# Two of eight routed experts run in a packed form with two matrix products a group, and GpSimd makes some of their weights' low parts

## The chip, the cores and the metric

One core of one Trainium2 chip runs the kernel. The metric is the device time in microseconds (us) of the slowest core, here the only one. The kernel before took 1445.33 us (median of 3 runs, 1445.06 to 1445.63). Engines are named as in the profile: PE multiplies matrices (PEld loads its stationary operand), DVE is VectorE, ACT is ScalarE, POOL is GpSimd, and SP issues most transfers.

## The reference

The reference is a two-layer decoder trunk: 256 tokens, model width 1024, all in float32. The change touches its last block, a feed-forward layer with eight experts of which each token takes two:

```python
logits = (x @ w_router).astype(jnp.float32)
top_logit, top_idx = lax.top_k(logits, 2)
gates = jax.nn.softmax(top_logit, axis=-1)
# for each expert e, over the tokens routed to it:
y = (jax.nn.silu(h @ w_gate[e]) * (h @ w_up[e])) @ w_down[e]
# w_gate, w_up: 1024 x 3584, w_down: 3584 x 1024, for each expert
out = zeros.at[rows_token].add(y * gate)      # then residual and a final rmsnorm
```

512 assignments fall on eight experts, 64 each on average. With the reference's own inputs (seed 0) the counts are 67, 51, 56, 55, 77, 75, 59 and 72. The order in which experts are worked on does not change the result, except for rounding.

## The kernel before

Every float32 weight is used as two parts that PE reads in a faster float32 form: `e_whi`, the rounded value, and `e_wlo`, the remainder. Activations are split in the same way. A product is then three matmuls, high x high, low x high and high x low (`three`, L1688 to L1690).

The weights of an expert come in 42 slots of 1 MB. Seven steps j handle 512 hidden columns each: two slots for the gate projection, two for the up projection and two for the down projection of the step before. A slot goes through a line of four:

- SP issues the load into one of 7 buffers `raw` (L440, L455); it waits until the low part of the slot 7 places earlier is done (`lo_ready`).
- ACT copies the slot into one of 6 buffers `e_whi` (L979), once PE has used the slot 6 places earlier.
- DVE subtracts and writes `e_wlo` (L1569).
- PE does 12 matmuls of 512 columns with it.

The order on each engine is written out by hand in its own block of code; semaphores tie the engines together. In a step PE does the gate product of step j, turns the hidden rows of step j-1 (`turn_hidden`, L2310), does the up product of step j and then the down product of j-1. ACT does the silu (L1002) and the high part of the turned hidden rows (L984), DVE the product gate x up (L1619) and their low part (L1582).

Up to 128 tokens of an expert sit in the 128 columns of the stationary operand. SP fetches an expert's tokens from `routed_rows` in DRAM during step 5 of the expert before (L449), PE turns them (L2304). POOL computes where each token's row goes, scatters the rows by indirect transfers (L551), stores each expert's result in `y_rows` (L559), and near the end gathers the rows of each token back (L568); DVE adds those, weighted, to the residual `xres` (`add_rows`, L1538). The last expert's result goes from PE's accumulator through a one-hot product (L2388) straight into `xres` (L1673), and the final norm follows. Where an expert has over 128 tokens a second pass over all experts runs; with these inputs it does not.

Of the kernel before, what the change touches and what calls it, by code (L numbers as in the profile page):

```python
# [24 lines left out]
P = 128  # L25
# [18 lines left out]
E_SPLIT = 6  # L44

# [53 lines left out]
def trunk(nc, x, mem, g_mix, g_ffn, w_mem_kv, w_out, w_in_a, w_gk_up, b_gk, g_gla, g_kv, w_kv, w_in_b,  # L99
# [10 lines left out]
    with ExitStack() as ctx:  # L110
# [15 lines left out]
        sb("act_pad", [P, 24])  # L126
# [12 lines left out]
        w_all = sb("w_r", [P, 184])[:, 0:KT * NE]  # L139
        w_r = w_all.rearrange("p (k e) -> p k e", k=KT)  # L140
        LOGITS = slice(NE * (KT - 1), NE * KT)

# [32 lines left out]
        h_hi, h_lo = ([buf[:, 4 * i:4 * i + 4, P:S] for i in range(2)] for buf in (act_hi, act_lo))  # L175

# [10 lines left out]
        y_mark = small[0:1, 28:29]  # L187
        cur_rank, cur_gate = small[:, 76:78], small[:, 78:80]
# [101 lines left out]
        ranked = sem("ranked")  # L290
# [23 lines left out]
        e_silu = sem("e_silu")  # L314
        e_hr = sem("e_hr")
        e_tr = sem("e_tr")
# [96 lines left out]
        def _(sp):  # L413
# [17 lines left out]
            def expert_loads(sweep):  # L431
                base = NPRE + sweep * NE * PER_EXPERT
                with sp.Fori(0, NE) as e:
                    u = 0
                    for j in range(STEPS + 1):
                        for wgt in ((w_exp_gate, w_exp_up) if j < STEPS else ()):
                            for half in range(2):
                                s = base + u
                                sp.wait_ge(lo_ready, e * PER_EXPERT + s - RAW + 1)
                                sp.dma_start(shaped(raw, s % RAW, 4, 512),  # L440
                                             wgt[0, e].rearrange("(k p) n -> p k n", p=P)
                                             [:, 4 * half:4 * half + 4, 512 * j:512 * j + 512])\
                                  .then_inc(raw_in[s % RAW], 16)
                                u += 1
                        if sweep == 0 and j == 5:
                            sp.wait_ge(rows_sent, 16 * 2 * TT)
                            sp.wait_ge(copy_sent, 16 * TT)
                            sp.wait_ge(disp, 2 * e + 2)
                            sp.dma_start(x_rows, routed_rows[P:].rearrange("(e p) d -> e p d", p=P)[e])\  # L449
                              .then_inc(x_rows_in, 16)  # L450
                        for half in (range(2) if j > 0 else ()):
                            s = base + u
                            sp.wait_ge(lo_ready, e * PER_EXPERT + s - RAW + 1)
                            k0 = 4 * (j - 1) + 2 * half
                            sp.dma_start(shaped(raw, s % RAW, 2, D),  # L455
                                         w_exp_down[0, e].rearrange("(k p) n -> p k n", p=P)[:, k0:k0 + 2, :])\
                              .then_inc(raw_in[s % RAW], 16)
                            u += 1

            expert_loads(0)  # L460
            sp.wait_ge(routed, 1)
            over = sp.value_load(flag[0:1, 0:1], min_val=0, max_val=S)
# [16 lines left out]
        def _(pool):  # L479
# [45 lines left out]
            pool.wait_ge(ranked, 1)  # L525
            iota8 = cst[:, C_IOTA:C_IOTA + NE].rearrange("p (o e) -> p o e", o=1).to_broadcast([P, TT, NE])
            nc.gpsimd.tensor_scalar(row1, route_rank[:, :, :], P - 0.5, 1.0e6, ALU.is_gt, ALU.mult)
            link(nc.gpsimd.tensor_scalar(row_of, iota8, float(P), None, ALU.mult))
# [27 lines left out]
            nc.gpsimd.tensor_copy(y_idx, rsc[:, 6:8, :, 0].rearrange("p c t -> p t c")).then_inc(y_idx_ready, 1)  # L556
            for i in range(NE - 1):
                pool.wait_ge(e_yo, 2 * (i + 2))
# [4 lines left out]
            pool.dma_start(gain[:, :], gains[-1].to_broadcast([P, D])).then_inc(gain_in, 16)  # L563
            pool.wait_ge(y_idx_ready, 1)
            for t in range(TT):
                pool.wait_ge(lo_ready, NPRE + NE * PER_EXPERT - RAW + t + 1)
                for c in range(2):
                    pool.indirect_dma_start(y_back[t][:, c, :], None, y_rows[:, :],  # L568
                                            bass.IndirectOffsetOnAxis(ap=y_idx[:, t, c:c + 1], axis=0),
                                            bounds_check=NE * P - 1, oob_is_err=True).then_inc(y_in[t], 16)  # L570

# [5 lines left out]
        def _(act):  # L577
# [384 lines left out]
            def evacuate_rows(i):  # L962

                act.wait_ge(slot_used, i * PER_EXPERT + NPRE)
                act.wait_ge(y_free, i + 1)
                for n in range(2):
                    ns = slice(512 * n, 512 * n + 512)
                    nc.scalar.activation(y_tok[:, ns], ps[:, 5 + n, :], ACT.Copy).then_inc(e_yo, 1)

            def experts(sweep):  # L970
# [16 lines left out]
                def expert(e, last):  # L987

                    for j in range(STEPS):
# [8 lines left out]
                        if j == 2 and (sweep or last):  # L998
                            act.wait_ge(oh_turned, e + 2 if sweep else 1)
                            nc.scalar.activation(ohT[:, :], ps[:, 7, 0:256], ACT.Copy).then_inc(ohT_ready, 1)  # L1000
# [10 lines left out]

                split_slots(0, 0, 1)
# [31 lines left out]
        def _(dve):  # L1044
# [434 lines left out]
            link(nc.vector.memset(flag[:, :], 0))  # L1479
            out_b_sums(0)  # L1480
# [26 lines left out]
            nc.vector.memset(rt[:, 30:31], 0.0).then_inc(ranked, 1)  # L1507

            def choice_inverse():
# [5 lines left out]
                link(nc.vector.tensor_reduce(rt[:, 24:25], ps[:, 4, 0:NE], AX.X, ALU.max))  # L1515
                nc.vector.tensor_copy(flag[0:1, 0:1], rt[0:1, 24:25]).then_inc(routed, 1)
# [14 lines left out]

            def add_rows(t, c):

                dve.wait_ge(gated, 1)
                dve.wait_ge(y_in[t], 32)
                if c:
                    dve.wait_ge(y_added, 2 * t + 1)
                nc.vector.scalar_tensor_tensor(out=xres[:, t, :], in0=y_back[t][:, c, :],  # L1538
                                               scalar=rt[:, 4 + 2 * c + t:5 + 2 * c + t], in1=xres[:, t, :],
                                               op0=ALU.mult, op1=ALU.add).then_inc(y_added, 1)  # L1540

            def experts(sweep):
# [45 lines left out]
                def expert(e, last):  # L1588

                    for j in range(STEPS):  # L1590
# [29 lines left out]
                        if j == STEPS - 1 and sweep == 0 and last:  # L1620
                            add_rows(0, 0)
# [5 lines left out]
                    hidden(e, STEPS - 1)  # L1627
                    if not last:
                        split_slots(e, PER_EXPERT + 1, 1)
                        gathered(sweep, e + 1)  # L1630
# [11 lines left out]
                with dve.Fori(0, NE - 1) as e:  # L1642
                    expert(e, False)
                expert(NE - 1, True)
                return remainder_y, add_tile

            remainder_y, add_tile = experts(0)
            add_rows(0, 1)
            add_rows(1, 0)
            add_rows(1, 1)  # L1650
            dve.wait_ge(routed, 1)
            over = dve.value_load(flag[0:1, 0:1], min_val=0, max_val=S)
            last_gates = cur_gate.rearrange("p (t o) -> p t o", o=1)
            with dve.If(over > P):
                remainder_y(NE)
                nc.vector.tensor_copy(last_gates, route_gate[:, :, NE:NE + 1]).then_inc(cur_done, 1)
# [5 lines left out]
            nc.vector.tensor_copy(last_gates, route_gate[:, :, NE:NE + 1]).then_inc(last_gate, 1)  # L1662
# [5 lines left out]
            dve.wait_ge(last_gate, 1)  # L1668
            for n in range(2):
# [15 lines left out]
        def _(pe):  # L1685
# [570 lines left out]
            def experts(sweep):  # L2256
# [49 lines left out]

                def turn_hidden(e, j):
# [30 lines left out]
                def expert(e, last):  # L2338
                    for j in range(STEPS):
# [8 lines left out]
                        if j == 2 and (sweep or last):  # L2348
                            pe.wait_ge(oh_ready, 2 * e + n_oh + 2 if sweep else 4)
# [6 lines left out]
                        elif j == 0:  # L2356
                            pe.wait_ge(routed, 1)
# [14 lines left out]
                with pe.Fori(0, NE - 1) as e:  # L2372
                    expert(e, False)
                expert(NE - 1, True)
# [3 lines left out]
            over = pe.value_load(flag[0:1, 0:1], min_val=0, max_val=S)  # L2378
# [58 lines left out]
```

## Time and profile before

| | us |
|---|---|
| median of 3 runs | 1445.33 |
| the profiled execution | 1445.62 |
| its span | 1443.8 |
| PE busy | 1416.1 (98%) |
| DVE busy | 1116.0 (77%) |
| ACT busy | 944.2 (65%) |
| POOL busy | 52.9 (4%) |
| DMA, mean | 309 GB/s |

The span is the stretch that the profile shows, 1.8 us less than the execution's own time. The expert stage runs from about 486 us to 1434 us. "Busy" of matmuls is modelled and overlaps, so the distance between the same place in two experts or steps says more than the busy sum.

### The profile page before, as it was taken

How to read it: one execution, taken by the hardware profiler on the slowest of the kernel's cores; microseconds unless marked ns; L12 is line 12 of the kernel's file. 1: busy time of each engine (PE TensorE's matmuls, PEld its weight loads, DVE VectorE, ACT ScalarE, POOL GpSimd, SP SyncE). 2: the span in 40 equal slices, each digit the busy share in tenths (PEclk: the TensorE clock that was granted, in tenths of full speed). 3: DMA queues.
4: the chain of work that ended last, by engine and by line, in shares of the span. 5: the costliest groups of instructions: out<-in, count | busy, mean ns of one | idle time of the engine just before them, and what ended most of it. 6: DMA issues, size and time to landing. Idle time of an engine off the chain costs nothing.

```text
span 1443.8 us, 19619 instructions
## 1 busy us (share of the span) xinstructions
PE 1416.1 (98%) x7392; PEld 1201.2 (83%) x7392; DVE 1116.0 (77%) x865; ACT 944.2 (65%) x866; POOL 52.9 (4%) x78
## 2 busy tenths in 40 slices
PE   9999999999999999999999999999999999999997
PEld 8887899998888888888888888888888888888886
DVE  4565544556776899798888889879889888988987
ACT  5654543434664877786777777767768767677773
POOL 1000100000000500000000000000000000000002
PEclk9999999999999999999999999999999999999999
DMA  9843675555531699999999999999999999999993
GB/s 278 270 146 118 238 243 177 194 185 189 190 117 59 236 396 396 397 393 395 394 361 397 394 346 392 398 345 388 397 392 351 395 393 345 393 398 363 392 397 128
DMA packets 205254, 446.72 MB, mean 309 GB/s; under 512 B 8449, under 2 KB 42401, under 8 KB 205201
## 3 DMA queue, kind: packets, MB, share of 16 engines
q1 hardware_dynamic: 200144, 428.34, 80.6%
q0 software_dynamic: 5056, 17.66, 3.6%
q8 instruction: 35, 0.57, 0.2%
q14 instruction: 19, 0.15, 0.0%
HBM read 432.86 MB, written 13.11 MB: 309 GB/s over the span
## 4 chain that ended last, share of the span: by engine, by line
PE 91%; ACT 3%; DVE 3%; DMA 1%; issue 0%; DVEq 0%; SPq 0%; ACTq 0%
PE ps L1688 29%; PE ps L1690 29%; PE ps L1689 29%; PE ps L2310 2%; DMA raw<-in_w_in_a_dram 1%; ACT w_hi L595 1%; DVE w_lo L1060 1%; PE ps L1839 0%; PE ps L1714 0%; PE ps L2304 0%; DVE small L1107 0%; ACT sc L639 0%; DVE act_lo L1073 0%; DMA H<-in_mem_dram 0%; PE ps L1823 0%
## 5 line engine op out<-in xcount | busy, mean ns | idle before, releaser
L1569 DVE TENSOR_TENSOR e_wlo<-raw,e_whi 128x2048 fp32r<-128x2048 f32 x336 | 752.0, 2284 | 102.2 <-ACT e_whi L979 102.1
L979 ACT ACTIVATE e_whi<-raw 128x2048 fp32r<-128x2048 f32 x336 | 622.5, 1915 | 48.7 <-PE ps L1690 27.6
L1688 PE MATMUL ps<-e_whi,act_hi 128*128 128x512 f32 x1344 | 529.4, 394 | 1.3 <-DVE act_lo L1527 1.3
L1690 PE MATMUL ps<-e_wlo,act_hi 128*128 128x512 f32 x1344 | 523.9, 390 | 0.0
L1689 PE MATMUL ps<-e_whi,act_lo 128*128 128x512 f32 x1344 | 523.2, 389 | 0.0
L1690 PEld LDWEIGHTS ps<-e_wlo,act_hi 128*128 128x128 f32 x1344 | 252.3, 188 | 53.4
L1688 PEld LDWEIGHTS ps<-e_whi,act_hi 128*128 128x128 f32 x1344 | 252.4, 188 | 52.5 <-DVE act_lo L1527 1.9
L1689 PEld LDWEIGHTS ps<-e_whi,act_lo 128*128 128x128 f32 x1344 | 252.6, 188 | 50.7
L1060 DVE TENSOR_TENSOR w_lo<-raw,w_hi 128x2048 fp32r<-128x2048 f32 (+3 forms) x69 | 148.7, 2167 | 119.8 <-ACT w_hi L595 119.5
L595 ACT ACTIVATE w_hi<-raw 128x2048 fp32r<-128x2048 f32 (+3 forms) x69 | 124.3, 1816 | 49.6 <-PE ps L1690 43.8
L984 ACT ACTIVATE act_hi<-ps 128x512 fp32r<-128x512 f32 x56 | 33.5, 599 | 158.7 <-PE ps L2310 158.7
L1688 PE MATMUL ps<-act_hi,w_hi 128*128 128x256 f32 (+2 forms) x440 | 124.8, 284 | 2.5 <-DVE act_lo L1073 2.5
L1689 PE MATMUL ps<-act_hi,w_lo 128*128 128x256 f32 (+2 forms) x440 | 124.3, 282 | 0.0
L1690 PE MATMUL ps<-act_lo,w_hi 128*128 128x256 f32 (+2 forms) x440 | 124.3, 282 | 0.0
L1688 PE MATMUL ps<-w_hi,act_hi 128*128 128x512 f32 (+1 forms) x272 | 98.9, 364 | 6.1 <-DVE act_lo L1073 4.2
L1690 PE MATMUL ps<-w_lo,act_hi 128*128 128x512 f32 (+1 forms) x272 | 96.0, 353 | 0.0
L1689 PE MATMUL ps<-w_hi,act_lo 128*128 128x512 f32 (+1 forms) x272 | 95.7, 352 | 0.0
L1688 PEld LDWEIGHTS ps<-act_hi,w_hi 128*128 128x128 f32 (+2 forms) x440 | 81.8, 186 | 3.9 <-issue 3.4
L1689 PEld LDWEIGHTS ps<-act_hi,w_lo 128*128 128x128 f32 (+2 forms) x440 | 81.8, 186 | 0.5
L1690 PEld LDWEIGHTS ps<-act_lo,w_hi 128*128 128x128 f32 (+2 forms) x440 | 81.8, 186 | 0.2
L1688 PEld LDWEIGHTS ps<-w_hi,act_hi 128*128 128x128 f32 x272 | 51.4, 189 | 14.7 <-DVE act_lo L1073 2.4
L1690 PEld LDWEIGHTS ps<-w_lo,act_hi 128*128 128x128 f32 x272 | 51.4, 189 | 7.3
(270 smaller groups left out, 967.3 us busy)
## 6 DMA issues: line engine op xcount, KB each, us to landing
raw<-in_w_exp_gate_dram SPq DMA_DIRECT2D x112, 1024.0 KB, 8.7
raw<-in_w_exp_up_dram SPq DMA_DIRECT2D x112, 1024.0 KB, 9.1
raw<-in_w_exp_down_dram SPq DMA_DIRECT2D x112, 1024.0 KB, 9.8
raw<-in_w_dense_gate_dram SPq DMA_DIRECT2D x11, 1024.0 KB, 5.4
raw<-in_w_dense_up_dram SPq DMA_DIRECT2D x11, 1024.0 KB, 5.8
raw<-in_w_dense_down_dram SPq DMA_DIRECT2D x11, 1024.0 KB, 6.3
raw<-in_w_out_dram SPq DMA_DIRECT2D x8, 1024.0 KB, 5.1
raw<-in_w_in_a_dram SPq DMA_DIRECT2D x7, 1024.0 KB, 12.2
```

What stands on the lines that cost most here:

```text
L595: nc.scalar.activation(w_hi[:, s % SPLIT, 0:kt * n], raw[:, s % RAW, 0:kt * n], ACT.Copy)\
L979: nc.scalar.activation(e_whi[:, (s - NPRE) % E_SPLIT, :], raw[:, s % RAW, :], ACT.Copy)\
L984: nc.scalar.activation(h_hi[j % 2], ps[:, 4, :].rearrange("p (m n) -> p m n", m=4), ACT.Copy)\
L1060: nc.vector.tensor_tensor(w_lo[:, s % SPLIT, 0:kt * n], raw[:, s % RAW, 0:kt * n], w_hi[:, s % SPLIT, 0:kt * n].bitcast(F32), ALU.subtract)\
L1569: nc.vector.tensor_tensor(e_wlo[:, r, :], raw[:, s % RAW, :], e_whi[:, r, :].bitcast(F32), ALU.subtract).then_inc(lo_ready, 1)
L1688: nc.tensor.matmul(dst, l_hi, r_hi, start=start, stop=False)
L1689: nc.tensor.matmul(dst, l_lo, r_hi, start=False, stop=False)
L1690: return nc.tensor.matmul(dst, l_hi, r_lo, start=False, stop=stop)
L2310: ins = nc.tensor.transpose(ps[:, 4, P * m:P * m + P], e_h[:, P * m:P * m + P], ident)
```

## The change

- Experts are put in order of their token count: expert 0 first, then by falling count, so that the two with the fewest tokens come last (indices 6 and 7 in this order, `FIRST_LIGHT = 6`). POOL computes the order from the counts; SP reads an expert's number from it before it loads that expert.
- These two "light" experts have room for 64 tokens (`LIGHT = 64`). The stationary operand holds the high parts of 64 tokens and beside them their low parts. One matmul with the weights' high part and one with their low part then give all four partial products; a group has 2 matmuls where it had 3. The two halves of the result lie in different rows and are added by a product with `fold`, two identity blocks on top of each other.
- Since silu needs the sum, ACT and DVE first copy gate and up unchanged (`light_gate`, `light_up`), PE folds and turns both in 8 small matmuls (`light_turn`), and silu, product and split come behind it on 256 columns.
- In steps 1 to 5 of a light expert POOL makes the low part of the step's fourth slot (the second of the down projection, slot `gate_end(j) + 3`). DVE waits for it and passes `lo_ready` on, to keep the order.
- The weighted adds of the gathered rows move from DVE to POOL, as a scaling and an add each, 8 instructions behind the last gather.
- Each engine has its own code for the light experts instead of the loop's.
- A count above 64 in a light expert, or above 128 elsewhere, starts the second pass.

The core of the diff:

```diff
+ # SP, sweep 0
+ loads(0, 0)
+ sp.wait_ge(routed, 1)
+ with sp.Fori(1, NE) as e:
+     loads(e, sp.value_load(order_of[0:1, bass.ds(e, 1)], min_val=0, max_val=NE - 1))
+ # POOL: before the row numbers; ranked was signalled by DVE ahead of its first weight slot
- pool.wait_ge(ranked, 1)
+ pool.wait_ge(counted, 1)
+ link(nc.gpsimd.tensor_scalar(key[:, :], count[:, :], float(NE), None, ALU.mult))
...
+ nc.gpsimd.tensor_copy(flag[0:1, 0:1], past[0:1, 0:1]).then_inc(routed, 1)
...
+ def low_parts(e):
+     for j in range(1, STEPS - 1):
+         s = NPRE + e * PER_EXPERT + gate_end(j) + 3
+         r = (s - NPRE) % E_SPLIT
+         pool.wait_ge(hi_ready, s + 1)
+         nc.gpsimd.tensor_tensor(e_wlo[:, r, :], raw[:, s % RAW, :], e_whi[:, r, :].bitcast(F32), ALU.subtract)\
+           .then_inc(pool_lo, 1)
...
+ # POOL, at the very end
+ for t in range(TT):
+     pool.wait_ge(y_in[t], 32)
+     for c in range(2):
+         nc.gpsimd.tensor_scalar(y_back[t][:, c, :], ..., ALU.mult).then_inc(y_scaled, 1)
+         nc.gpsimd.tensor_tensor(xres[:, t, :], xres[:, t, :], y_back[t][:, c, :], ALU.add).then_inc(y_added, 1)
+ # ACT, a step of a light expert
+ split_slots(e, up, 2)
+ split_slots(e, up + 2, 1)
+ light_silu(e, j - 1)
+ light_gate(e, j)
+ light_high(e, j - 1)
+ split_slots(e, up + 3, 2)
+ split_slots(e, up + 5, 1)
+ # DVE, a step of a light expert (passed_on waits for POOL's slot)
+ split_slots(e, up, 2)
+ light_product(e, j - 1)
+ split_slots(e, up + 2, 1)
+ light_low(e, j - 1)
+ passed_on(e, j)
+ light_up(e, j)
+ split_slots(e, up + 4, 2)
+ # DVE, before the last additions to xres
+ dve.wait_ge(y_added, 2 * TT)
+ # PE, a slot of a light expert
+ for kk in range(4):
+     k = 4 * half + kk
+     nc.tensor.matmul(bank, xg_hi[:, k, :], hi[:, kk, :], start=k == 0, stop=False)
+     ins = nc.tensor.matmul(bank, xg_hi[:, k, :], lo[:, kk, :], start=False, stop=k == KT - 1)
+ # PE, between the last two experts: the result of the light expert before is folded
+ def fold_rows():
+     pe.wait_ge(y_raw, 2)
+     for n in range(2):
+         ins = nc.tensor.matmul(ps[0:LIGHT, 5 + n, :], fold, y_tok[:, 512 * n:512 * n + 512], start=True, stop=True)
```

DVE in the last expert, before: a step is six `e_wlo`, one `act_lo` and one `e_h`, and the adds to `xres` come behind the last step.

```order
L1569 TENSOR_TENSOR e_wlo<-raw,e_whi 128x2048 [waits hi_ready] x2
L1619 TENSOR_TENSOR e_h<-e_h,ps 128x512 [waits slot_used,e_silu]
L1569 TENSOR_TENSOR e_wlo<-raw,e_whi 128x2048 [waits hi_ready] x4
L1582 TENSOR_TENSOR act_lo<-ps,act_hi 128x4x128 [waits e_hi]
L1569 TENSOR_TENSOR e_wlo<-raw,e_whi 128x2048 [waits hi_ready] x2
L1619 TENSOR_TENSOR e_h<-e_h,ps 128x512 [waits slot_used,e_silu]
L1538 SCALAR_TENSOR_TENSOR xres<-raw,small,xres 128x1024 [waits y_in0,gated]
```

DVE in a light expert, after (`H` holds the up product and the folded rows; the MEMSET is `passed_on`):

```order
L1713 TENSOR_TENSOR e_wlo<-raw,e_whi 128x2048 [waits hi_ready]
L1775 TENSOR_TENSOR act_hi<-H,act_hi 128x4x64 [waits e_hi]
L1799 MEMSET small 1x1 [waits pool_lo]
L1795 COPY H<-ps 128x512 [waits slot_used]
L1713 TENSOR_TENSOR e_wlo<-raw,e_whi 128x2048 [waits hi_ready] x4
L1771 TENSOR_TENSOR H<-H,ps 128x256 [waits l_silu]
L1713 TENSOR_TENSOR e_wlo<-raw,e_whi 128x2048 [waits hi_ready]
L1775 TENSOR_TENSOR act_hi<-H,act_hi 128x4x64 [waits e_hi]
L1799 MEMSET small 1x1 [waits pool_lo]
```

One of six `e_wlo` has left DVE, and in its place stands a wait for POOL, with the copy of the up product and all later slots behind it. POOL from the gather to its end, after (before, the four gathers were the last; `raw` and `xres` are what they fill and what is added to):

```order
L639 TENSOR_TENSOR e_wlo<-raw,e_whi 128x2048 [waits hi_ready] x5
L656 DMA raw<-y_rows,idx 128x1024 [waits lo_ready,y_idx_ready]
L656 DMA raw<-y_rows,idx 128x1024
L656 DMA raw<-y_rows,idx 128x1024 [waits lo_ready]
L656 DMA raw<-y_rows,idx 128x1024
L662 TENSOR_SCALAR raw<-raw,small 128x1024 [waits y_in0]
L665 TENSOR_TENSOR xres<-xres,raw 128x1024 [waits y_scaled]
L662 TENSOR_SCALAR raw<-raw,small 128x1024 [waits y_added]
L665 TENSOR_TENSOR xres<-xres,raw 128x1024 [waits y_scaled]
L662 TENSOR_SCALAR raw<-raw,small 128x1024 [waits y_in1,y_added]
```

The additions now stand in one line on POOL, each behind the one before. POOL's routing before its scatter of the rows, which had 13 instructions from `ranked` on, has 43 from `counted` on; nearly all wait for the one ahead of them.

## Rows read from the trace of the kernel before

**Rows 1.** The page, parts 2 and 4: GB/s in 40 slices; shares of the chain.

```profile
GB/s 278 270 146 118 238 243 177 194 185 189 190 117 59 236 396 396 397 393 395 394 361 397 394 346 392 398 345 388 397 392 351 395 393 345 393 398 363 392 397 128
...
PE 91%; ACT 3%; DVE 3%; DMA 1%; issue 0%; DVEq 0%; SPq 0%; ACTq 0%
```

**Rows 2.** Busy time by stretch: one expert; DVE's `e_wlo` line alone.

```profile
700.00:818.60 118.60, 118.60 (x542) 98.09 (x541) 103.03 (x59) 86.24 (x60) 0.67 (x2) 1.00 1.02 385
...
487.20:546.00 58.80, 51.95 (x24) 1.00 1.02 384
```

**Rows 3.** The page, part 5: count, busy us, mean ns of one, idle before and its releaser.

```profile
L1569 DVE TENSOR_TENSOR e_wlo<-raw,e_whi 128x2048 fp32r<-128x2048 f32 x336 | 752.0, 2284 | 102.2 <-ACT e_whi L979 102.1
L979 ACT ACTIVATE e_whi<-raw 128x2048 fp32r<-128x2048 f32 x336 | 622.5, 1915 | 48.7 <-PE ps L1690 27.6
```

**Rows 4.** The chain that ended last: start us, us, what.

```profile
568.00 0.44 PE ps L2310 x4
...
1189.92 0.87 PE ps L2304 x8
...
1308.56 0.87 PE ps L2304 x8
1331.21 0.44 PE ps L2310 x4
1348.01 0.44 PE ps L2310 x4
```

**Rows 5.** Timeline of DVE: start us, us, line, operation, count, idle before and its releaser.

```profile
487.28 4.51 DVE L1569 TENSOR_TENSOR e_wlo<-raw,e_whi 128x2048 fp32r<-128x2048 f32 x2
...
1204.16 4.49 DVE L1569 TENSOR_TENSOR e_wlo<-raw,e_whi 128x2048 fp32r<-128x2048 f32 x2 [6.34 <-ACT e_whi L979]
...
1390.23 8.89 DVE L1569 TENSOR_TENSOR e_wlo<-raw,e_whi 128x2048 fp32r<-128x2048 f32 x4
...
1418.83 4.49 DVE L1569 TENSOR_TENSOR e_wlo<-raw,e_whi 128x2048 fp32r<-128x2048 f32 x2 [1.60 <-ACT e_whi L979]
...
1434.23 2.73 DVE L1673 SCALAR_TENSOR_TENSOR xres<-ps,small,xres 128x512 f32<-128x512 f32 x4
```

**Rows 6.** Timeline of ACT: the wait at the start of the seventh expert, the last copies.

```profile
1201.73 0.60 ACT L1002 ACTIVATE e_h<-ps 128x512 f32<-128x512 f32 x1 [4.27 <-PE ps L1690]
...
1432.86 0.60 ACT L1038 ACTIVATE y_hi<-ps 128x512 fp32r<-128x512 f32 x1 [0.70 <-PE ps L1690]
```

**Rows 7.** Timeline of POOL.

```profile
482.57 0.79 POOL L535 TENSOR_TENSOR rsc<-rsc 128x16 f32<-128x16 f32 x3
...
489.73 2.15 POOL L546 TENSOR_TENSOR route_gate<-rsc 128x16 f32<-128x16 f32 x1
...
497.91 2.50 POOL L551 DMA_INDIRECT routed_rows<-H,idx  x1 [0.30 <-issue]
...
1407.41 2.88 POOL L568 DMA_INDIRECT raw<-y_rows,idx  x1 [83.67 <-DVE e_wlo L1569]
...
1414.91 1.90 POOL L568 DMA_INDIRECT raw<-y_rows,idx  x1 [0.30 <-issue]
```

**Rows 8.** Groups of POOL by line and shape: count, busy us, mean ns of one.

```profile
L503 POOL MEMSET T<- 128x1024 f32 x1 | 1.0, 974 | 0.0
...
L532 POOL TENSOR_TENSOR rsc<-rsc 128x16 f32<-128x16 f32 x1 | 0.2, 227 | 0.0
...
L544 POOL TENSOR_TENSOR small<-small 128x2 f32<-128x2 f32 x1 | 0.2, 197 | 0.0
```

**Rows 9.** Timeline of SP's queue: the row fetch in the first expert.

```profile
548.72 2.31 SPq L449 DMA_DIRECT2D H<-routed_rows  x1
```

**Rows 10.** Lines L551, L568 and L455 by themselves: time from issue to landing.

```profile
DMA to landing us min/median/max: 7.5/9.0/9.4
...
DMA to landing us min/median/max: 5.5/5.8/6.8
...
DMA to landing us min/median/max: 4.9/9.8/15.4
```

More of the change, by code:

```diff
@@ L432, in expert_loads, with loads @@
                 base = NPRE + sweep * NE * PER_EXPERT
-                with sp.Fori(0, NE) as e:
+                def loads(e, x):
                     u = 0
@@ L1627, in expert, with light_product, light_low @@
                     hidden(e, STEPS - 1)
+                    if not last:
+                        split_slots(e, PER_EXPERT + 1, 1)
+                        gathered(sweep, e + 1)
+                def light_product(e, j):
+                    dve.wait_ge(l_silu, (e - FIRST_LIGHT) * STEPS + j + 1)
+                    nc.vector.tensor_tensor(h_T, s_T, ps[:, 4, 256:512], ALU.mult).then_inc(l_prod, 1)
+                def light_low(e, j):
+                    dve.wait_ge(e_hi, e * STEPS + j + 1)
+                    nc.vector.tensor_tensor(h_hi[j % 2][:, :, LIGHT:P], h_T.rearrange("p (m n) -> p m n", m=4),
+                                            h_hi[j % 2][:, :, 0:LIGHT].bitcast(F32), ALU.subtract).then_inc(e_lo, 1)
@@ new lines, in light_up, with passed_on, light_expert @@
+                def light_up(e, j):
+                    dve.wait_ge(slot_used, e * PER_EXPERT + base + gate_end(j) + 2)
+                    nc.vector.tensor_copy(e_u, ps[:, 2 + j % 2, :]).then_inc(e_hr, 1)
+                def passed_on(e, j):
+                    dve.wait_ge(pool_lo, (e - FIRST_LIGHT) * (STEPS - 2) + j)
+                    nc.vector.memset(y_mark2, 0.0).then_inc(lo_ready, 1)
+                def light_expert(e, last):
+                    for half in range(2):
+                        pack(e, half)
+                    split_slots(e, 2, 2)
+                    if last:
+                        light_one_hot()
+                    split_slots(e, 4, 2)
+                    light_up(e, 0)
+                    for j in range(1, STEPS):
+                        up = gate_end(j)
+                        split_slots(e, up, 2)
+                        light_product(e, j - 1)
+                        split_slots(e, up + 2, 1)
+                        light_low(e, j - 1)
+                        if j < STEPS - 1:
+                            passed_on(e, j)
+                        else:
+                            split_slots(e, up + 3, 1)
+                        light_up(e, j)
+                        split_slots(e, up + 4, 2)
+                    if not last:
+                        split_slots(e, PER_EXPERT, 1)
+                    light_product(e, STEPS - 1)
+                    light_low(e, STEPS - 1)
@@ L2347, in expert @@
                             scatter(e + 1, 1)
[L2348 to L2349 removed]
+                        if j == 2 and sweep:
+                            pe.wait_ge(oh_ready, 2 * e + n_oh + 2)
                             for t in range(TT):
```

270 lines of the change are left out of this document (219 added, 51 removed).

## The prediction

> **What bounds the kernel now.** I read the chain of waits first: PE holds 91% of it, and within the experts it is only matmuls [rows 1, 4]. The same turn of token rows stands at 1189.92 and 1308.56, so an expert takes 118.64 us; two hidden turns are 16.80 us apart, which is a step of six slots [rows 4]. The turn is 0.44 us of it, so a matmul comes every (16.80 - 0.44) / 72 = 0.227 us and a slot costs PE 12 x 0.227 = 2.73 us. The busy time by stretch comes next, to see who is second: in one expert of 118.6 us DVE is busy 103.0 and ACT 86.2, POOL 0.7, and 385 GB/s are moved [rows 2]. The slices of the page stand at about 396 GB/s wherever no expert begins [rows 1]; at that pace a 1 MB slot takes 2.65 us. So four engines work at nearly one pace: PE 2.73 us a slot, DMA 2.65, DVE 2.28, ACT 1.92 [rows 3]. Taking a third of PE's work away can win little before another takes over; the question is which, and what it does.
>
> **PE's part.** A light slot has 8 matmuls, 1.81 us, 0.92 less. Over 84 slots that is 77 us, but it does not reach the end: a step would be 10.9 us on PE plus a fold, and neither DMA (15.9 us) nor DVE allows it. DVE alone with six slots would need 6 x 2.2 (back to back four take 8.89 [rows 5]) plus the copy of up (0.6, a little under 2.73 / 4 as in the last additions [rows 5]), product and low part on 256 columns (0.4 each, estimated from 0.6 on 512), together 14.6. DMA would then set the pace, under the present 16.8.
>
> **The slot that POOL takes.** Here the order on the engines decides. DVE can't run ahead of its wait in `passed_on`. I follow one cycle from the end of `light_product`: ACT may now do `light_high` (0.4) and only then the copy of the slot that POOL is to work on (1.9); with a handoff 2.4 us. POOL's subtraction takes P, and 0.2 goes for its two handoffs. Then DVE copies up (0.6), makes four `e_wlo` (8.85) and the next product (0.4). DVE's one slot and `light_low` in between (2.6) fit beside ACT's 2.4, so POOL's P stands open on DVE. The cycle is 2.4 + 0.2 + P + 0.6 + 8.85 + 0.4 = 12.45 + P. PE and SP wait behind DVE.
>
> P is not in the trace: no two-input operation of 2048 elements ran on POOL. From below: a memset of 1024 took 0.974 us, one stream [rows 8], so 1.95 us for 2048. From above: two streams in and one out at that pace, 5.8 us. Between them, two tensor-tensor operations on 16 and on 2 elements took 227 and 197 ns, a slope of 2.1 ns an element, and 4.6 us at 2048. That is the nearest row in kind, though the lever is short; I take 4.4. A cycle is then 16.85 us, where the step of before was 16.80.
>
> The Trainium skill (GPSIMD Engine Reference, "Performance versus the Vector engine") gives 4497 ns for such an addition of 2048 elements on GpSimd against 2293 ns on VectorE. The trace bears out the second with 2284 ns [rows 3] and shows nothing of the first; with it the sum below would be 1 us more.
>
> **Do POOL and DVE wait for each other?** POOL's L546 is a 16-element operation that takes 2.15 us and ends at 491.88, just behind the pair of `e_wlo` that ends at 491.79, while three such operations in a gap of DVE took 0.79 together [rows 5, 7]. So a POOL operation is held for as long as DVE's two-input one. Whether a long one on POOL holds DVE equally no row shows. In the cycle it matters little, as DVE is waiting anyway; at the end it does.
> The Trainium skill (SBUF — State Buffer, "The single rule") says it goes both ways, whichever starts first: by that rule the slot given away costs DVE more than it saves, in any order of the instructions.
>
> **The sum**, along DVE. Seventh expert: slots 4 and 5 began at 1204.16, behind ACT's wait for PE's first two slots [rows 5, 6]; PE is 2 x 0.92 faster, so 1202.35. Two `e_wlo` 4.45, up 0.6, two more 4.4, product 0.4: 1212.2. Five cycles of 16.85: 1296.45. To slot 41: 2.2 + 0.4 + 2.2 + 0.6 + 4.45 = 9.85, so 1306.3. The same place before is 1423.32 - 118.64 = 1304.7 (end of the last pair [rows 5]). Eighth: slot 0 2.2, product 0.4, ACT's high part and copy 2.4, slot 1 2.2, gathered rows 1.2, pack 0.25 make 8.65. Then the fold stands in the way: PE's four slots 7.25 and the two folding matmuls (in plain float32; between 0.45 as fast ones and four times that; I take 1.8), ACT's evacuation 1.1, its next copy 1.9, handoffs 0.3, then two `e_wlo` 4.45, up 0.6, two 4.4 and product 0.4: 30.85 in all, where before the same stretch takes 27.6 (1204.16 + 4.45 + 0.6 + 4.45 + 118.64 - 1304.7). That is 1337.15; five cycles, 1421.4; 9.85, 1431.25. POOL's first tail operations hold the last two slots for 1.4: 1432.65, against 1423.32 before.
>
> **The end.** PE is close behind now: product, high, low and handoffs 1.5, two slots 3.6, one hold by POOL 1.2, so 6.3 us after that slot, and the last additions could start 1.7 later (1434.23 against 1432.55 before [rows 5, 6]), 8.0 in all. But they now wait for POOL's additions. The gathers start 15 us before the last slot is done (six slots and the small ones), take 9.4 to issue as 1407.41 to 1416.81, and the first pair lands 5.8 after its second issue [rows 7, 10], some 5.5 us before the last slot. Then four scalings (1.0 from the memset) and four additions (P/2 = 2.2), handoffs 0.8 and two `e_wlo` ahead of them (4.4) make 18.0: 12.5 us behind the last slot, 4.5 later than PE's side. Before, DVE did them under PE's matmuls. Additions start at 1432.65 + 12.5 = 1445.15, before at 1434.23: 10.9 later. The rest stays as it is.
>
> **The routing on POOL.** 43 chained operations begin only at 487.2, with DVE on `e_wlo` in 51.95 of the next 58.8 us [rows 2]. One gets through with each of the 23 or so slots; a gap of DVE takes one to three, at 0.26 to 0.3 each [rows 7]. That ends near 546. The scatter's last issue comes 6.0 behind them (497.91 - 491.88) and lands 9.4 later [rows 7, 10]: 561, where SP asked for the rows at 548.72 [rows 9]. The weight load behind it lands at 562.8 + 4.9 [rows 10], its low part is done at 572.3, and PE wants it after the turn at 568.00 and two more slots [rows 4], at 573.9. So 12 us of wait are covered with 1.6 us left. I put 1 us down, bounds 0 and 10. The expert number that SP reads costs no more than a few of its idle microseconds once an expert.
>
> Together 10.9 + 1.0 = 11.9 on the profiled execution's 1445.62, which is 0.3 above the median: 1457.5 us.
>
> **The rivals.**
> - POOL's part is cheap. With P = 2.3, as on DVE, ten cycles lose 2.1 each and the four additions 1.05: 1457.5 - 21 - 4.2 = 1432. DMA about permits it: 84 loads and 1.5 more for rows take 226.6 us at 2.65, and DVE's way would be 237.3 + 9.3 - 21 = 225.6. For it: the memset's pace. Against: two inputs, and the slope of the small operations. The sign turns at P = 4.4 - 11.9 / 12 = 3.4.
> - POOL is slower than I take it, or DVE and POOL hold each other in every cycle: 5.8 us gives 1457.5 + 14.0 + 2.8 = 1474. For it: three streams; against: the slope.
> - The routing comes too late. Were each of the 43 operations to wait for a whole DVE slot (2.55 us apart), it would end at 597, the rows land at 612, and PE would stand for 48 us: 1505. It decides from 563 us on (561 + 1.6). For it: only 1.6 us of cover. Against: small operations pass in DVE's gaps, and DVE stops when loads stop.
> - The change doesn't do what it says, because a light expert has over 64 tokens and all eight run twice. The counts of 51 and 55 speak against it; it would be over 2300 us.
>
> **How the numbers follow.** The forecast with its near range (1450 to 1466) has 0.6, the cheap POOL 0.2 (times 1431 to 1442), the slower POOL 0.1, late routing 0.09, the second pass 0.01. The range of 8 in 10 goes from 1438 to 1470. 0.2%, 2.9 us, is about what a measurement of this kernel can tell: faster 0.19, same 0.05, slower 0.76.
>
> **What would show it.** POOL's 2048-element row near 4.4 us, ten of them, each with DVE idle and the wait before the MEMSET put down to POOL; hidden turns of the last two experts about 16.9 us apart; PE idle in them; the last `xres` additions waiting for POOL; SP's row fetch near 561. It is wrong if P is under 3.4 us, if POOL starts while DVE still has slots to do, or if PE stands in the first expert.

## The result and the profile after

The changed kernel takes 1467.47 us (median of 4 runs, 1467.0 to 1468.95), the kernel before 1445.19 in the same comparison (4 runs, 1444.14 to 1445.63). The ratio is 1.0158, with an interval of 1.0142 to 1.0174: 22.3 us slower. The forecast was 1457.5 with a range of 1438 to 1470, so the time lies inside the range, and 1.5 us above the near range of 1450 to 1466 that had a chance of 0.6.

| | before | after |
|---|---|---|
| the profiled execution | 1445.62 | 1467.45 |
| its span | 1443.8 | 1465.6 |
| PE busy | 1416.1 (98%) | 1389.5 (95%) |
| DVE busy | 1116.0 (77%) | 1096.4 (75%) |
| POOL busy | 52.9 (4%) | 165.4 (11%) |

PE has less work and the kernel takes longer, so the time must be in waits. Parts 2 and 4 of the page after the change, beside [rows 1]:

```profile
POOL 1000100000000790000000000000000002211247
...
GB/s 281 260 144 115 277 218 188 202 194 176 170 115 30 328 393 368 393 394 397 391 363 395 395 347 397 393 350 393 398 350 390 397 363 369 374 380 310 364 366 68
...
PE 77%; POOL 6%; DVE 6%; ACT 4%; issue 3%; DMA 3%; SPq 1%; DVEq 0%; ACTq 0%; POOLq 0%
```

PE's share of the chain is 77% where it was 91%. In the slices of the last two experts (363, 369, 374, 380 and on) the transfers no longer reach 396 GB/s.

POOL's groups of the changed kernel (count, busy us, mean ns of one, idle before and its releaser). L639 is the low part, L662 and L665 are the scaling and the addition near the end:

```profile
L639 POOL TENSOR_TENSOR e_wlo<-raw,e_whi 128x2048 fp32r<-128x2048 f32 x10 | 46.3, 4626 | 121.8 <-ACT e_whi L1075 121.8
L662 POOL TENSOR_SCALAR raw<-raw,small 128x1024 f32<-128x1024 f32 x4 | 13.3, 3330 | 0.3
L665 POOL TENSOR_TENSOR xres<-xres,raw 128x1024 f32<-128x1024 f32 x4 | 9.6, 2407 | 0.3
```

P is 4.63 us where [rows 3] have 2.284 for the same work on DVE. The Trainium skill (GPSIMD Engine Reference, "Performance versus the Vector engine") gives 4497 ns for an addition of this size; the subtraction in the trace is 0.13 us above it.

One cycle on DVE in the seventh expert after the change (start us, us, what, idle before), to be held against the steady six `e_wlo` of before:

```profile
1213.14 0.41 DVE L1771 TENSOR_TENSOR H<-H,ps 128x256 f32<-128x256 f32 x1
1213.47 2.29 DVE L1713 TENSOR_TENSOR e_wlo<-raw,e_whi 128x2048 fp32r<-128x2048 f32 x1
1215.67 0.42 DVE L1775 TENSOR_TENSOR act_hi<-H,act_hi 128x256 fp32r<-128x256 f32 x1
1220.56 0.69 DVE L1795 COPY H<-ps 128x512 f32<-128x512 f32 x1 [4.47 <-issue]
1220.58 0.06 DVE L1799 MEMSET small<- 1x1 f32 x1
1221.17 8.89 DVE L1713 TENSOR_TENSOR e_wlo<-raw,e_whi 128x2048 fp32r<-128x2048 f32 x4
1230.61 0.42 DVE L1771 TENSOR_TENSOR H<-H,ps 128x256 f32<-128x256 f32 x1 [0.55 <-ACT H L1110]
```

And what POOL does in the same stretch:

```profile
1215.90 4.63 POOL L639 TENSOR_TENSOR e_wlo<-raw,e_whi 128x2048 fp32r<-128x2048 f32 x1 [10.17 <-ACT e_whi L1075]
1233.37 4.63 POOL L639 TENSOR_TENSOR e_wlo<-raw,e_whi 128x2048 fp32r<-128x2048 f32 x1 [12.85 <-ACT e_whi L1075]
```

POOL begins at 1215.90, just behind DVE's slot (done at 1215.76), and ends at 1220.53; DVE goes on at 1220.56. The profile books these 4.47 us to "issue". That POOL ends 0.03 us before DVE goes on, and 0.04 us before it in the next cycle (1238.00 and 1238.04), shows whose wait it is. POOL itself waits 10 to 13 us in each cycle. So the two engines take turns.

### The profile page after: what moved, and what is told of

Read it like the earlier page. It is cut to its first block, busy times and chain, and to the rows that moved or that the text cites. A ratio compares the mean times of both kernels' runs of the same rounds, so it can differ in the third digit from the quotient of the medians.

```text
span 1465.6 us, 19160 instructions
## 1 busy us (share of the span) xinstructions
PE 1389.5 (95%) x7228; PEld 1170.5 (80%) x7228; DVE 1096.4 (75%) x881; ACT 945.3 (65%) x882; POOL 165.4 (11%) x125
## 4 chain that ended last, share of the span: by engine, by line
PE 77%; POOL 6%; DVE 6%; ACT 4%; issue 3%; DMA 3%; SPq 1%; DVEq 0%; ACTq 0%; POOLq 0%
PE ps L1896 21%; PE ps L1898 21%; PE ps L1897 21%; PE ps L2523 3%; PE ps L2524 3%; DVE e_wlo L1713 3%; PE ps L2545 2%; DMA raw<-in_w_exp_down_dram 2%; PE ps L2547 2%; PE ps L2534 1%; PE ps L2589 1%; DMA raw<-in_w_mem_kv_dram 1%; POOL raw L662 1%; ACT w_hi L691 1%; ACT e_whi L1075 1%
## 5 line engine op out<-in xcount | busy, mean ns | idle before, releaser
L1713 DVE TENSOR_TENSOR e_wlo<-raw,e_whi 128x2048 fp32r<-128x2048 f32 x326 | 733.3, 2297 | 90.4 <-ACT e_whi L1075 90.4
L1896 PE MATMUL ps<-e_whi,act_hi 128*128 128x512 f32 x1008 | 397.2, 394 | 1.6 <-DVE act_lo L1681 1.3
L1898 PE MATMUL ps<-e_wlo,act_hi 128*128 128x512 f32 x1008 | 393.0, 390 | 0.0
L1897 PE MATMUL ps<-e_whi,act_lo 128*128 128x512 f32 x1008 | 392.4, 389 | 0.0
L1896 PEld LDWEIGHTS ps<-e_whi,act_hi 128*128 128x128 f32 x1008 | 189.3, 188 | 40.4 <-DVE act_lo L1681 1.9
L1898 PEld LDWEIGHTS ps<-e_wlo,act_hi 128*128 128x128 f32 x1008 | 189.2, 188 | 40.0
L1897 PEld LDWEIGHTS ps<-e_whi,act_lo 128*128 128x128 f32 x1008 | 189.4, 188 | 38.0
L1080 ACT ACTIVATE act_hi<-ps 128x512 fp32r<-128x512 f32 x42 | 25.1, 598 | 120.4 <-PE ps L2589 120.4
L2523 PE MATMUL ps<-e_whi,act_hi 128*128 128x512 f32 x224 | 93.5, 417 | 7.6 <-DVE e_wlo L1713 7.5
L2524 PE MATMUL ps<-e_wlo,act_hi 128*128 128x512 f32 x224 | 90.5, 404 | 0.0
L2545 PE MATMUL ps<-e_whi,act_hi 128*128 128x512 f32 x112 | 54.3, 485 | 33.0 <-DVE small L1799 24.4
```

The costliest lines, as they stand in the source:

```text
L1080: nc.scalar.activation(h_hi[j % 2], ps[:, 4, :].rearrange("p (m n) -> p m n", m=4), ACT.Copy)\
L1713: nc.vector.tensor_tensor(e_wlo[:, r, :], raw[:, s % RAW, :], e_whi[:, r, :].bitcast(F32), ALU.subtract).then_inc(lo_ready, 1)
L1896: nc.tensor.matmul(dst, l_hi, r_hi, start=start, stop=False)
L1897: nc.tensor.matmul(dst, l_lo, r_hi, start=False, stop=False)
L1898: return nc.tensor.matmul(dst, l_hi, r_lo, start=False, stop=stop)
L2523: nc.tensor.matmul(bank, xg_hi[:, k, :], hi[:, kk, :], start=k == 0, stop=False)
```

## The experiments

### The two parts of POOL's work, each by itself

Three kernels put POOL's parts back on DVE: the low parts, the additions, and both. They and the fourth below ran on one chip beside 13 runs of the kernel before (1444.36 us).

```diff
  # e1_dve_low, and in e3_dve_both: POOL makes no low parts, DVE makes all six
-     if i >= FIRST_LIGHT:
-         low_parts(i)
...
-     if j < STEPS - 1:
-         passed_on(e, j)
-     else:
-         split_slots(e, up + 3, 1)
+     split_slots(e, up + 3, 1)
```
```diff
  # e2_dve_adds, and in e3_dve_both: DVE adds behind its last light_low, POOL's 8 instructions go
-         nc.gpsimd.tensor_scalar(y_back[t][:, c, :], ..., ALU.mult).then_inc(y_scaled, 1)
-         nc.gpsimd.tensor_tensor(xres[:, t, :], xres[:, t, :], y_back[t][:, c, :], ALU.add).then_inc(y_added, 1)
...
+     nc.vector.scalar_tensor_tensor(out=xres[:, t, :], in0=y_back[t][:, c, :], scalar=..., in1=xres[:, t, :],
+                                    op0=ALU.mult, op1=ALU.add).then_inc(y_added, 1)
```

> DVE makes all low parts of the light experts again, one edit; POOL keeps the additions at the end. The order theory (DVE stands for all of POOL's 4.6 us in each of ten cycles of 17.1 us): a cycle falls to what DVE needs by itself, 14.6 to 14.9 us, so DVE's last slot comes 22 to 24 us earlier, POOL's additions then end some 18 us behind it, and the time is 1445 to 1449 us. The rival, that transfers set the pace once POOL is out (six slots of 2.65 us, 15.9 a cycle): some 12 us are won, 1453 to 1457 us. If the fallen matmul clock set the cycle: no change of the hidden turns' distance from 17.1 us, 1465 us or more.

> DVE makes the four weighted additions behind its last low part, as before the change; POOL keeps its ten low parts. The theory that POOL's chain at the end costs 6.3 us behind PE (its additions end at 1456.0, PE's side could start them at 1449.7) and 2.1 us more by holding DVE's last two low parts (8.03 us for both instead of 4.49): 8 us less, 1458 to 1461 us. The rival, that the gathers are late anyway because POOL comes to them late: the additions wait for the second pair of rows, and only 2 to 4 us are won, 1463 to 1466 us.

> Both edits: POOL has neither low parts nor additions, the two-product form of the light experts stays. If the two costs stand one behind the other and DVE's own order sets the cycle (14.6 to 14.9 us): 22 to 24 and 8 us less than the changed kernel, 1431 to 1438 us, faster than the kernel before. If transfers set the pace (15.9 us a cycle): 1445 to 1449 us. If the two-product form itself were what is slow (fold, clock, waits at the experts' start), it would stay above 1450 us.

| kernel | low parts | additions | us, median | ratio, interval |
|---|---|---|---|---|
| changed | POOL | POOL | 1467.47 | 1.0158, 1.0142 to 1.0174 |
| e2_dve_adds | POOL | DVE | 1457.48 | 1.0080, 1.0063 to 1.0097 |
| e1_dve_low | DVE | POOL | 1450.91 | 1.0044, 1.0027 to 1.0061 |
| e3_dve_both | DVE | DVE | 1442.90 | 0.9987, 0.9977 to 0.9996 |

Taken away from the changed kernel, the low parts on POOL are worth 1.14% (16.5 us) and the additions 0.78% (11 us); both together 1.71% (25 us), which is less than the sum of the two, so they overlap by some 3 us. With neither the change is 1.9 us faster than before by the ratio, with an interval of 0.6 to 3.3 us. So the two things given to POOL carry the whole loss, and the low parts the larger half. e1_dve_low came out between the two expectations, e2_dve_adds a little below its own, e3_dve_both at neither: 5 us above the one by DVE's order, 2 us below the one by transfers.

DVE in e3_dve_both, cycles without POOL:

```profile
1228.37 0.42 DVE L1768 TENSOR_TENSOR H<-H,ps 128x256 f32<-128x256 f32 x1
...
1242.88 0.42 DVE L1768 TENSOR_TENSOR H<-H,ps 128x256 f32<-128x256 f32 x1
...
1257.42 0.42 DVE L1768 TENSOR_TENSOR H<-H,ps 128x256 f32<-128x256 f32 x1
...
1273.67 0.42 DVE L1768 TENSOR_TENSOR H<-H,ps 128x256 f32<-128x256 f32 x1 [1.68 <-ACT H L1099]
```

A cycle between two products takes 14.51 us here, as the 14.6 of the prediction; POOL's slot made it 17.47 in the rows above. Ten cycles at this pace would save some 26 us. But only the first three cycles of an expert run at it; in the seventh expert the fourth takes 16.25 and the fifth 15.87, in the eighth 15.63 and 16.07. All ten take 151.1 us where those of the changed kernel take 171.0, those of e1_dve_low 152.8, and of the 18.2 us won there 16.5 reach its end. The waits of ACT between 1220 and 1420 us in e3_dve_both (us in total, times, longest) say where the rest is:

```profile
ACT H L1099 <- PE ps L2532: 15.2, 7, 3.6
ACT e_whi L1064 <- DMA raw<-in_w_exp_down_dram: 11.7, 10, 2.3
ACT e_whi L1064 <- DMA raw<-in_w_exp_up_dram: 6.4, 10, 0.8
ACT gain L1053 <- PE ps L2555: 4.9, 1, 4.9
ACT e_whi L1064 <- DMA raw<-in_w_exp_gate_dram: 3.5, 6, 0.8
```

Three of the lines are loads that arrive too late, 21.6 us in all. The chain of waits says the same: from 1332 to 1420 us a third of it (33.0%) is transfers of `raw`, such as

```profile
1376.34 12.68 DMA raw<-in_w_exp_down_dram
```

and the changed kernel's chain has no transfer in that stretch. From 1220 to 1300 us 395 GB/s are moved, before's pace. So, by the trace, transfers set the pace once DVE doesn't. The first line is ACT's wait for the fold and turn of each step, and no run tells how much of it hangs on the loads. The line on `gain` is the fold between the experts, taken up below.

### Do DVE and POOL run at the same time?

In the changed kernel DVE stands while POOL works. Here DVE copies up and makes the next slot's low part first, and waits for POOL after that.

```diff
  # e4_one_ahead: DVE, steps 1 to 5 of a light expert
-     passed_on(e, j)
-     light_up(e, j)
-     split_slots(e, up + 4, 2)
+     light_up(e, j)
+     one_ahead(e, j)          # the low part of slot gate_end(j) + 4, then the wait for POOL
+     split_slots(e, up + 5, 1)
```

> POOL keeps its low parts, but DVE copies up and makes the next slot's low part before it waits for POOL, so that this work could run beside POOL's. If a two-input operation of DVE is held for as long as POOL's runs: only the copy of up (0.6 us, from PSUM) is won in each of ten cycles, 1460 to 1463 us, and the low part that stands ahead starts only when POOL's ends. If DVE and POOL can run together: 2.8 us a cycle, down to the transfers' 15.9 us a cycle or below, 1440 to 1456 us.

It took 1499.49 us, ratio 1.0375 (1.0357 to 1.0392). DVE and POOL in one cycle (L1808 is the subtraction that was moved ahead):

```profile
1235.20 0.42 DVE L1773 TENSOR_TENSOR H<-H,ps 128x256 f32<-128x256 f32 x1 [3.88 <-ACT H L1112]
...
1239.72 5.03 DVE L1808 TENSOR_TENSOR e_wlo<-raw,e_whi 128x2048 fp32r<-128x2048 f32 x1 [0.51 <-ACT e_whi L1077]
...
1255.60 0.42 DVE L1773 TENSOR_TENSOR H<-H,ps 128x256 f32<-128x256 f32 x1 [3.99 <-ACT H L1112]
```
```profile
1237.97 4.63 POOL L641 TENSOR_TENSOR e_wlo<-raw,e_whi 128x2048 fp32r<-128x2048 f32 x1 [15.65 <-ACT e_whi L1077]
```

POOL holds on from 1237.97 to 1242.60 at its usual 4.63. DVE's operation starts in the middle of it and ends at 1244.75, 2.15 behind POOL's end: its own length, as if it had begun only then. All ten took 4.98 to 5.04 us. So a long two-input operation on POOL holds DVE's, as [rows 5, 7] had shown the other direction. The Trainium skill (SBUF — State Buffer, "Who interferes with whom", under "The single rule") says this for both directions, and these rows bear it out; a pair of operations at the end of the kernel, told under "Open" below, does not fit it.

Both expectations missed the size. The hold was there, but a cycle is 20.40 us. POOL's slot is passed on 2.2 us later than in the changed kernel, and PE, which had waited for it, then needs longer than DVE; DVE stands another 3.9 us for `H` before each product. Part of why PE needs so long shows in the section on the hardware.

### The fold, and how far it goes without POOL

e5_fold_late is e3_dve_both with ACT's copies of slots 4 and 5 ahead of its wait for the fold. e6_four_light is e5_fold_late with four light experts, since the counts 59, 56, 55 and 51 all fit.

```diff
  # e5_fold_late: ACT at the start of a light expert
+     split_slots(e, 4, 2)
...
          act.wait_ge(y_folded, e - FIRST_LIGHT)
...
-     split_slots(e, 4, 2)
  # e6_four_light
- FIRST_LIGHT = 6
+ FIRST_LIGHT = 4
```

> As the kernel in which DVE makes all low parts and the additions (1442.9 us), with one more change: ACT copies slots 4 and 5 of a light expert before it waits for the folded result of the light expert before, where it waited first. In that kernel DVE stands 7.1 us at the start of the last expert, and ACT 4.9 us for the fold. If this stall is what the last expert loses, 3 to 5 us come back: 1438 to 1440 us, and the stretch from slot 1 to slot 4 on DVE shortens by as much. If the transfers set the pace there (the cycles ended at about 16 us, with ACT waiting for raw), the gain is given back by waits for transfers: 1441.5 to 1443.5 us.

> The kernel e5_fold_late with four light experts in place of two (counts 59, 56, 55 and 51 all fit in 64). If the limit of a light expert without POOL's part is the transfers, an expert takes 45.1 MB at 396 GB/s, 114 us, where a packed-less one takes 118.6: two more experts bring 8 to 9 us, so 1429 to 1433 us. If the boundaries between experts (fold, first slots, PE at its lower clock) cost as much as the steps give, it is within 2 us of e5_fold_late.

e5_fold_late: 1440.85 us, ratio 0.9974 (0.9965 to 0.9983) against 1444.83 of before (15 runs in this comparison). This interval and that of e3_dve_both overlap a little, so the gain in time is at the edge of what these runs can tell; the rows show it more clearly. e6_four_light: 1433.01, ratio 0.9919 (0.9905 to 0.9932).

DVE's first pair behind the fold, in e3_dve_both and then in e5_fold_late:

```profile
1320.76 4.49 DVE L1702 TENSOR_TENSOR e_wlo<-raw,e_whi 128x2048 fp32r<-128x2048 f32 x2 [7.07 <-ACT e_whi L1064]
```
```profile
1314.20 4.50 DVE L1702 TENSOR_TENSOR e_wlo<-raw,e_whi 128x2048 fp32r<-128x2048 f32 x2 [1.21 <-ACT e_whi L1064]
```

The pair comes 6.6 us earlier (0.7 of it were there at the start of the expert). The last product of the expert is at 1416.62 in e5_fold_late and at 1419.95 in e3_dve_both, 3.3 earlier, and the medians differ by 2.1 (0.13%). So the stall was real, and more than half of what its end gave was taken back. In that expert (1310 to 1420 us) ACT waits 20.4 us for loads of `raw` in e5_fold_late and 11.6 in e3_dve_both, which points to the transfers. The result is between the two expectations, nearer to the second.

In e6_four_light the last product of the seventh expert and that of the eighth stand 115.25 us apart:

```profile
1295.34 0.41 DVE L1768 TENSOR_TENSOR H<-H,ps 128x256 f32<-128x256 f32 x1
...
1410.59 0.41 DVE L1768 TENSOR_TENSOR H<-H,ps 128x256 f32<-128x256 f32 x1
```

A full expert takes 118.64 [rows 4], so a light one saves 3.4 us. Two more save 6.8 by that, and 7.8 were measured, just under the 8 to 9 of the first expectation. A window of 120 us within the light experts of e6_four_light (PE, PEld, DVE, ACT, POOL busy, PEclk, DMA share, GB/s):

```profile
1080.00:1200.00 120.00, 107.14 (x485) 81.38 (x484) 109.40 (x71) 94.58 (x74) 1.16 (x3) 0.97 1.04 395
```

395 GB/s is the pace of before's fullest slices, 396 [rows 1], and from 1200 to 1310 us it is the same: by this the light expert runs at the pace of the transfers. e6_four_light is the best version found, 12 us below the kernel before.

### The cover of the routing

```diff
  # e7_more_links: POOL, in the routing
+ for _ in range(8):
+     link(nc.gpsimd.tensor_scalar(key[:, :], key[:, :], 0.0, None, ALU.add))
```

> The changed kernel with 8 more small operations in POOL's chain of routing (each adds 0 to the key; the result is unchanged). 43 operations took 58 us, so 8 more put the rows some 11 us later. If the cover was nearly used up (a turn of rows came 1.4 us late in the changed kernel), all of it reaches the end: 1476 to 1480 us, and the turn at 1191.30 moves to about 1202. If there is more cover than I worked out, it stays within 2 us of 1467.

It took 1471.53 us (2 runs, ratio 1.0185, 1.0167 to 1.0204), about 4 more. The eight operations took 10.19 us, but later ones found more gaps of DVE, and the chain ended 7.3 later (551.22 in place of 543.93). The last scatter then landed 4.8 us after its issue where it took 7.0 in the changed kernel. So SP's fetch of the rows moved only by 4.9, here from the changed kernel and from e7_more_links:

```profile
558.63 0.34 SPq L470 DMA_DIRECT2D H<-routed_rows  x1
```
```profile
563.55 0.34 SPq L470 DMA_DIRECT2D H<-routed_rows  x1
```

The turn of the token rows, same two kernels in the chain of waits:

```profile
598.14 0.87 PE ps L2512 x8
...
1191.30 0.88 PE ps L2512 x8
```
```profile
604.52 0.87 PE ps L2514 x8
...
1197.68 0.87 PE ps L2514 x8
```

4.9 us more before the fetch are 6.4 more in PE, so nothing of the cover was left, and the light experts gave 2 back. The expectation of 11 us later was wrong in how the chain grows; that the cover is used up was right. PE stands 6.13 us in e7_more_links before 578.53, and its matmuls then start 0.43 us apart until 584.67 and 0.23 apart only behind that, which adds to the wait:

```profile
578.53 0.79 PE L1898 MATMUL ps<-e_whi,act_hi 128*128 128x512 f32 x1 [6.13 <-DVE act_lo L1728]
```

### What the scaling costs

```diff
  # e8_fixed_scale: leaves the weights of the experts out of the gathered part
- nc.gpsimd.tensor_scalar(y_back[t][:, c, :], y_back[t][:, c, :], rt[:, 4 + 2 * c + t:5 + 2 * c + t], None,
+ nc.gpsimd.tensor_scalar(y_back[t][:, c, :], y_back[t][:, c, :], 0.5, None,
```

> The changed kernel with POOL's four scalings by a constant 0.5 in place of each token's weight from small (this leaves the weights of the experts out of the result). If the 2.85 us of an unheld scaling of 1024 elements come from the scalar that is read per partition, it falls towards 1.0 us (the memset of the same size), and the end comes about 6 us earlier: 1461 us. If the operation itself costs that much, it stays at 2.8 us and the time at 1467.

POOL's last scaling in the changed kernel and in e8_fixed_scale:

```profile
1450.69 2.84 POOL L662 TENSOR_SCALAR raw<-raw,small 128x1024 f32<-128x1024 f32 x1
```
```profile
1447.20 2.77 POOL L662 TENSOR_SCALAR raw<-raw 128x1024 f32<-128x1024 f32 x1
```

The scalar read per partition costs 0.07 us; the rest is the operation, so the expected fall towards 1.0 us did not come. The two runs of this kernel, 1463.96 and 1470.03 us, lie too far apart to tell its time from the changed kernel's.

## Why the prediction was right in sign and 10 us short

The steps of the sum along DVE, with where each stood in the prediction and in the changed kernel's profile:

| step | predicted | measured | off |
|---|---|---|---|
| first product of the seventh expert ends (routing in) | 1213.2 | 1213.55 | +0.35 |
| five cycles | 84.25 | 86.13 | +1.9 |
| to slot 41 | 9.85 | 9.7 | -0.1 |
| start of the eighth, with the fold | 30.85 | 32.5 | +1.6 |
| five cycles | 84.25 | 84.84 | +0.6 |
| to the last slot, held by POOL | 11.25 | 13.3 | +2.0 |
| from there to the last additions | 12.5 | 16.0 | +3.5 |

Together 9.9, which is the distance of the profiled 1467.45 from 1457.5.

**The cycle** was right in mechanism and nearly in size. 12.45 + 4.63 is 17.08; measured are 17.23 and 16.97. P at 4.4 was 0.23 short, 2.3 us over ten cycles, nearly all of what the cycles missed. e1_dve_low shows that the slot on POOL is what costs.

**The routing** cost 1.4 us where 1 was put down. That it comes late by little was right; the place was not, nor was the landing: SP's fetch came at 558.63, not at 561, as the last scatter landed 7.0 us behind its issue and not 9.4. PE did not wait at 573.9. It stood 0.26 us before 589.76 and 1.96 us before 594.73, the second time at the end of a chain from a load issued behind the rows; here that load and PE's wait:

```profile
574.51 15.30 DMA raw<-in_w_exp_down_dram
594.73 0.66 PE L2589 MATMUL ps<-cst,e_h 128*128 128x128 f32 x4 [1.96 <-DVE e_h L1758]
```

Its hidden turn before that stood at 583.41, 1.24 us earlier than before the change, which gave part of the wait back. By the prediction's own sign, "if PE stands in the first expert", this part was wrong, though it cost only 0.4 us more than was put down.

**The fold** was taken at 1.8 us and the stretch at 30.85. ACT's wait for the two folding matmuls is

```profile
1327.60 1.07 ACT L1064 ACTIVATE gain<-ps 64x512 f32<-64x512 f32 x2 [4.89 <-PE ps L2557]
```

and DVE stands 7.14 for the copy behind them (to 1330.50), then another 1.46 for `H` before its product. ACT's evacuation is the predicted 1.1, and PE's fold took 1.93, near the 1.8. What was missed is the 1.46, PE being late with up and gate. It had stood 5.29 us for DVE's slots, and all 12 matmuls behind that wait start 0.43 us apart, not 0.23:

```profile
1332.85 0.80 PE L2523 MATMUL ps<-e_whi,act_hi 128*128 128x512 f32 x1 [5.29 <-DVE e_wlo L1713]
```

**The end** holds the largest error, in the scaling that was taken at 1.0 us from the memset [rows 8]. POOL's tail in the changed kernel:

```profile
1432.38 2.87 POOL L662 TENSOR_SCALAR raw<-raw,small 128x1024 f32<-128x1024 f32 x1
1435.33 2.52 POOL L665 TENSOR_TENSOR xres<-xres,raw 128x1024 f32<-128x1024 f32 x1
1437.95 4.76 POOL L662 TENSOR_SCALAR raw<-raw,small 128x1024 f32<-128x1024 f32 x1
...
1453.62 2.34 POOL L665 TENSOR_TENSOR xres<-xres,raw 128x1024 f32<-128x1024 f32 x1
```

Unheld it is 2.85, so four cost 7.4 more than taken, and the four additions 0.8 more. One scaling was held by DVE's last `e_wlo`, for 1.9 us where 4.4 had been put down for both slots, which gave 2.5 back. DVE's own two were held too, for 2.0 more than the 1.4 allowed:

```profile
1431.98 8.03 DVE L1713 TENSOR_TENSOR e_wlo<-raw,e_whi 128x2048 fp32r<-128x2048 f32 x2
...
1456.04 2.73 DVE L1881 SCALAR_TENSOR_TENSOR xres<-ps,small,xres 128x512 f32<-128x512 f32 x4 [6.58 <-POOL xres L665]
```

POOL started 2.1 us earlier against the last slot than predicted (7.6 instead of 5.5), which gave a part back too: 7.4 + 0.8 - 2.5 - 2.1 is 3.6, the 3.5 of the table. The mis-sized scaling is the largest wrong term of the sum; that the end was off by 3.5 and not by 8 is luck, since the shorter hold and POOL's earlier start happened to go the other way. The additions start at 1456.04, before at 1434.23 [rows 5]: 21.8 of the 21.83 us between the two profiled executions. The predicted wait on POOL was there, 6.58 us, where 4.5 were put down.

**The rivals.** The cheap POOL was given 1432, and e3_dve_both, which has DVE's own 2.3 us in place of POOL's, shows that this was too good even on its own terms: 1442.9. The slower POOL (5.8 us, 1474) did not come either: P, 0.23 above the 4.4, accounts for some 3 of the 9.9 us, in the ten cycles and the additions. The bound of the transfers was worked out as one sum over both experts and came out level with DVE's way. But with both at one pace a stall of DVE can't be caught up later. For the fold the rows of e5_fold_late show it, and 2.1 us in time at the edge of the noise; for the other 9 us I have only the long fourth and fifth cycles, the chain and ACT's waits for loads, and no run that changed the transfers alone. The mutual hold existed, with the exception told under "Open", but within the cycles it cost nothing, since DVE stands there anyway; it decided the last two slots and e4_one_ahead. The late routing did not happen, as small operations pass in DVE's gaps. Under 64 tokens the experts stayed, and no second pass ran.

## What to carry to other kernels

Work moved from VectorE to GpSimd is a gain only if the two don't take turns: here one subtraction of 2048 elements took 4.6 us in place of 2.3, and the two engines took turns whether VectorE waited for it by a semaphore or was held by it. Taking a third of an engine's work away moves the end only up to the next limit, here by the trace the transfers, 3.4 us in 118.6; find that limit first, and put no new wait on the engine that is second. At the end of a kernel, where nothing covers it, price each kind of operation by a row of its own kind: a memset's rate was 2.9 times too fast for a scaling.

## What the runs showed of the hardware that was not expected

**PE's clock falls in the light experts.** The windows from 1220 to 1300 us of the changed kernel and of e1_dve_low (last columns: granted clock, DMA share, GB/s):

```profile
1220.00:1300.00 80.00, 69.33 (x302) 54.72 (x303) 60.02 (x44) 54.38 (x42) 19.05 (x5) 0.89 1.01 372
```
```profile
1220.00:1300.00 80.00, 71.46 (x344) 55.16 (x344) 76.72 (x48) 62.91 (x47) 0.00 (x0) 1.00 1.04 395
```

The granted clock is 0.89 where PE waits once a cycle for POOL's slot, and 1.00 where it doesn't. The single matmuls behind such a wait, in the changed kernel:

```profile
1366.10 0.79 PE L2545 MATMUL ps<-e_whi,act_hi 128*128 128x512 f32 x1 [2.53 <-DVE small L1799]
...
1367.12 0.63 PE L2545 MATMUL ps<-e_whi,act_hi 128*128 128x512 f32 x1
1367.55 0.63 PE L2547 MATMUL ps<-e_wlo,act_hi 128*128 128x512 f32 x1
...
1369.59 0.39 PE L2524 MATMUL ps<-e_wlo,act_hi 128*128 128x512 f32 x1
1369.81 0.39 PE L2523 MATMUL ps<-e_whi,act_hi 128*128 128x512 f32 x1
```

They start 0.43 us apart and, 3 us later, 0.23: PE goes at 1.2 GHz behind 2.53 us of idling and comes back to 2.4. Seven matmuls at 0.2 more each are 1.4 us, which PE can mostly hide in the changed kernel. What is not hidden are DVE's waits for `H`, 0.55 falling to 0.16 in the five cycles of the seventh expert (1.5 in all), and 1.46 behind the fold, where the prediction had none. In e4_one_ahead the granted clock of the same window is 0.83 and PE became the path: behind 4.63 us of idling its matmuls start 0.43 apart from 1245.58 to 1250.70. No run changed the clock by itself, so its share of the time is read from these rows, not shown by an experiment.

**POOL's small operations** take 0.2 to 0.3 us in a gap of DVE and 2.1 to 2.4 behind a subtraction of DVE: the 43 of the routing took 57.9 us (486.02 to 543.93), as predicted near 546.

**Open** is why DVE's first of the last two `e_wlo` was held in part while it had started 0.40 us ahead of POOL's scaling. The two took 8.03 us together, the longest 4.43, so the other 3.6 in place of 2.3, while the scaling took its usual 2.87: here the one that began first was held. In the last expert of e4_one_ahead a scaling from 1462.00 took 3.96 and an `e_wlo` from 1463.23 took 3.12, both longer than alone. The second of the two `e_wlo` is no riddle: it ends 2.16 us behind POOL's addition (1437.85 and 1440.01), as in e4_one_ahead.
